# Expert weights through one ring of nine 2 MB slots in place of head and tail buffers of 1 MB, in a transformer layer with a top-4-of-32 mixture of experts

## What is computed

```python
def expert_block(args):
    xb, e = args
    g = xb @ w_gate[e] + b_gate[e]
    u = xb @ w_up[e] + b_up[e]
    g = jnp.minimum(g, SWIGLU_LIMIT)
    u = jnp.clip(u, -SWIGLU_LIMIT, SWIGLU_LIMIT)
    a = g * jax.nn.sigmoid(SWIGLU_ALPHA * g) * (u + 1.0)
    return a @ w_down[e] + b_down[e]
```

## Time and profile before

| | |
|---|---|
| median of 3 runs | 1187.4 us (1185.58 to 1191.16) |
| the profiled execution, own time | 1189.11 us |
| its span in the profile | 1187.2 us |
| TensorE busy | 1116.5 us, 94% |
| DVE busy | 306.2 us, 26% |
| ACT busy | 199.2 us, 17% |
| DMA, all queues | 438.73 MB, 370 GB/s over the span |

### The profile page before, as it was taken

The page is one execution under the profiler, slowest core; times in us unless marked ns, Lnnn a source line. Parts: engine busy times, 40 slices in busy tenths (PEclk is TensorE's granted clock), DMA queues, the critical chain, the costliest instruction groups (busy, mean ns, idle before and its releaser), DMA issues.

```text
span 1187.2 us, 13964 instructions
## 1 busy us (share of the span) xinstructions
PE 1116.5 (94%) x5368; PEld 523.6 (44%) x5368; DVE 306.2 (26%) x719; ACT 199.2 (17%) x339; POOL 5.5 (0%) x12
## 2 busy tenths in 40 slices
PE   7999999999999999999999999999999999999996
PEld 5888888533433333333333333333333333333332
DVE  7666665431111111111111111111121111111112
ACT  5345443011111111110111111101111111111111
POOL 1000000000000000000000000000000000000000
PEclk9999999999999999999999999999999999999998
DMA  9644327889999999799999999999999999999995
GB/s 351 230 168 152 121 94 289 363 332 378 421 421 421 421 422 421 282 423 421 423 422 422 421 422 421 423 421 422 421 423 421 423 421 423 421 423 421 423 421 213
DMA packets 71923, 438.73 MB, mean 370 GB/s; under 512 B 7356, under 2 KB 8408, under 8 KB 22744
## 3 DMA queue, kind: packets, MB, share of 16 engines
q1 hardware_dynamic: 71880, 438.36, 90.2%
q10 hardware_dynamic: 16, 0.00, 0.0%
HBM read 437.29 MB, written 1.05 MB: 369 GB/s over the span
## 4 chain that ended last, share of the span: by engine, by line
PE 82%; DMA 12%; ACT 3%; issue 1%; DVE 1%; SPq 0%; POOL 0%; DVEq 0%; POOLq 0%; ACTq 0%
PE ps L874 48%; DMA wu<-in_w_up_dram 11%; PE ps L901 5%; PE ps L838 4%; PE ps L862 4%; PE ps L598 4%; PE ps L784 2%; PE ps L636 2%; PE ps L661 2%; PE ps L628 2%; ACT gates L541 1%; PE ps L708 1%; PE ps L709 1%; PE ps L710 1%; DMA xs<-in_x_dram 1%
## 5 line engine op out<-in xcount | busy, mean ns | idle before, releaser
L874 PE MATMUL ps<-wd,o_t 128*64 128x512 f32 x1024 | 228.5, 598 | 22.8 <-issue 12.5
L874 PE MATMUL ps<-wu,gates 128*64 128x512 f32 x640 | 146.1, 594 | 6.2 <-DMA wu<-in_w_up_dram 6.2
L1264 DVE TENSOR_SCALAR gates<-ps 128x512 f32<-128x512 f32 x32 | 22.1, 692 | 486.9 <-PE ps L874 486.9
L874 PEld LDWEIGHTS ps<-wd,o_t 128*64 128x64 f32 x1024 | 78.6, 137 | 150.5 <-issue 137.4
L874 PE MATMUL ps<-wg,gates 128*64 128x512 f32 x512 | 113.0, 592 | 0.0
L874 PEld LDWEIGHTS ps<-wu,gates 128*64 128x64 f32 x640 | 50.1, 137 | 96.3 <-issue 75.6
L874 PE MATMUL ps<-attn,gates 128*64 128x512 f32 x384 | 89.3, 600 | 0.0
L553 ACT ACTIVATE gates<-ps 64x512 f32<-64x512 f32 x64 | 37.9, 592 | 233.1 <-PE ps L874 232.3
L874 PEld LDWEIGHTS ps<-wg,gates 128*64 128x64 f32 x512 | 43.3, 137 | 66.5 <-issue 64.0
L901 PE MATMUL ps<-gates,o_t 128*128 128x512 f32 x128 | 59.2, 605 | 10.2 <-ACT o_t L537 8.9
L862 PE MATMUL ps<-bias_tab,work 128*64 128x512 f32 x256 | 67.1, 595 | 0.7 <-DVE gates L1258 0.7
(11 more groups left out here) (163 smaller groups left out, 1083.8 us busy)
## 6 DMA issues: line engine op xcount, KB each, us to landing
wd<-in_w_down_dram SPq DMA_DIRECT2D x128, 1024.0 KB, 15.0
wu<-in_w_up_dram SPq DMA_DIRECT2D x80, 1024.0 KB, 22.3
wg<-in_w_gate_dram SPq DMA_DIRECT2D x64, 1024.0 KB, 17.5
attn<-in_w_gate_dram SPq DMA_DIRECT2D x32, 1024.0 KB, 18.9
v_tok<-in_w_gate_dram SPq DMA_DIRECT2D x16, 1024.0 KB, 21.8
work<-in_w_gate_dram SPq DMA_DIRECT2D x16, 1024.0 KB, 23.6
xn<-in_w_up_dram SPq DMA_DIRECT2D x16, 1024.0 KB, 25.5
attn<-in_w_up_dram SPq DMA_DIRECT2D x16, 1024.0 KB, 25.8
```

The lines of the kernel that those rows point to most:

```text
L874: mm = pe.matmul(ps[SLOTS * h:SLOTS * h + SLOTS, bank, :], lhs[:, k, :], w[:, k - 2 * j, 512 * h:512 * h + 512], start=(k == 0 and not bia ...
```

## The change

The 19 places of 1 MB become a ring of nine slots of 2 MB (18 MB): `attn[:, 2048:6144]`; the end of `work` and the start of `v_tok`, which now lie side by side; the halves of `wg`, `wu` and `wd`; and `xn` with `h_t`. A piece is 2 MB, 6 for an expert, two for each matrix. Piece number n of all 192 goes to slot n % 9, is issued in the order of use, and waits only until piece n - 9 is used. Partition p holds four successive rows of a matrix, 16 KB in one run (`RUN = 4`); the DMAs number half as many.

With four rows in a partition the transposes take every fourth column, a step of 4 floats (`every_fourth`), in `turn_rows`, `turn_residual` and for `rows_f`; their number is the same. The waits of DVE and ACT on `pieces_used` are rewritten in the new pieces: that for `pick_biases` is met when half of the up product is done (2 MB), where it was a quarter (1 MB). The loops over the pairs are unrolled on TensorE, DVE and ACT, and SP's loops too; the waits there are on constants. `g_fin` is loaded to `attn[:, 0:1024]` before the router's logits are done, and the result is written to `wg`.

```diff
-PIECES = 12
-HEAD = 7
-AHEAD_PAIRS = 4
+PIECES = 6
+RING = 9
+RUN = 4
...
+        work_at = nc.sbuf_base + (-nc.sbuf_base) % 32
         work = sb("work", [P, 4608])
+        v_tok = sb("v_tok", [P, NB, 1280])
+        slot_wv = nc.alloc_sbuf_tensor_at("slot_wv", [P, RUN, D], F32, offset=work_at + 2560 * 4)
+        slot_xh = nc.alloc_sbuf_tensor_at("slot_xh", [P, RUN, D], F32, offset=xn_at)
...
-        g_fin = msk[:, 0:D]
+        g_fin = attn[:, 0:D]
+        y_out = wg[:, 0:NB, :]
...
+        ring = [attn[:, 8 * SEQ:24 * SEQ].rearrange("p (k c) -> p k c", c=D), slot_wv]
+        ring += [t[:, 4 * j:4 * j + 4, :] for t in (wg, wu, wd) for j in range(2)] + [slot_xh]
+
+        def every_fourth(ap, r):
+
+            return ap[:, :].rearrange("p (c r) -> p r c", r=RUN)[:, r, :]
...
-        expert_v = [t[0].rearrange("e (j p r) f -> e j p r f", p=P, r=2) for t in (w_gate, w_up, w_down)]
+        expert_v = [t[0].rearrange("e (j p r) f -> e j p r f", p=P, r=RUN) for t in (w_gate, w_up, w_down)]
...
+            def piece(n, e):
+
+                m, j = n % PIECES // 2, n % 2
+                sp.dma_start(ring[n % RING][:], expert_v[m][e, j]).then_inc(ld_ring[n % RING], 16)
...
             sp.wait_ge(row_max, n_soft[N_UNITS])
-            piece(1, 1, 1)
+            piece(0, 0)
             sp.wait_ge(pv_done, N_UNITS // 2)
-            piece(2, 1, 1)
-            piece(3, 1, 1)
+            piece(1, 0)
...
             sp.wait_ge(oproj_done, KT)
...
+            for n in range(2, 6):
+                piece(n, 0)
+            for n in range(6, 8):
+                sp.wait_ge(wo_used, 2 * (n - 5))
+                piece(n, 1)
+            sp.dma_start(g_fin, ln_final_g.rearrange("(a d) -> a d", a=1).broadcast_to([P, D])).then_inc(ld_gfin, 16)
             sp.wait_ge(logit_done, NB)
...
+            piece(8, 1)
+            for n in range(RING, E * PIECES):
+                sp.wait_ge(pieces_used, n - RING + 1)
+                piece(n, n // PIECES)
...
-                    at = 512 * h + 2 * P * (k // 2)
-                    mm = turn(ps[:, 6 + h, P * k:P * k + P], every_second(xs[:, b, at:at + 2 * P], k % 2))
+                    mm = turn(ps[:, 6 + h, P * k:P * k + P], every_fourth(xs[:, b, 512 * h:512 * h + 512], k))
...
             def turn_rows(bank, rows_ap):
                 for j in range(4):
-                    mm = turn(ps[:, bank, P * j:P * j + P], every_second(rows_ap[:, 2 * P * (j // 2):2 * P * (j // 2) + 2 * P], j % 2))
+                    mm = turn(ps[:, bank, P * j:P * j + P], every_fourth(rows_ap, j))
                 return mm
...
+                for j in range(2):
+                    n = (E if again is not None else e) * PIECES + 2 * m + j
+                    pe.wait_ge(ld_ring[n % RING], (n // RING + 1 if again is None else again + (n // RING + 1)) * 16)
+                    for r in range(RUN):
+                        k = RUN * j + r
                         for h in range(2):
                             mm = pe.matmul(ps[SLOTS * h:SLOTS * h + SLOTS, bank, :], lhs[:, k, :],
-                                           w[:, k - 2 * j, 512 * h:512 * h + 512],
+                                           ring[n % RING][:, r, 512 * h:512 * h + 512],
                                            start=(k == 0 and not bias), stop=(k == KT - 1), skip_group_check=True)
                     mm.then_inc(pieces_used, 1)
...
-            with pe.Fori(1, E // 2 - 1) as i:
+            for i in range(1, E // 2 - 1):
                 pair(i)
...
-                    dve.wait_ge(pieces_used, n * PIECES + 5)
+                    dve.wait_ge(pieces_used, n * PIECES + 3)
```

More of the change, by code:

```diff
@@ L219, in layer @@
         ld_wo, ld_wout, ld_gfin, ld_bdn = sem("ld_wo"), sem("ld_wout"), sem("ld_gfin"), sem("ld_bdn")
-        ld_main = [sem(f"ld_main{q}") for q in range(PIECES)]
-        ld_second = [sem(f"ld_second{q}") for q in range(HEAD)]
+        ld_ring = [sem(f"ld_ring{s}") for s in range(RING)]
         wo_used = sem("wo_used")
@@ L368, in _ @@
             sp.wait_ge(oproj_done, KT)
-            piece(4, 1, 1)
-            for q in range(7):
-                piece(q, 0, 0)
-            for q in range(8, PIECES):
-                sp.wait_ge(wo_used, q - 7)
-                piece(q, 0, 0)
-            piece(5, 1, 1)
-            sp.wait_ge(logit_done, NB)
-            piece(6, 1, 1)
-            def head(i, item):
-                for q in range(HEAD):
-                    sp.wait_ge(pieces_used, i * (2 * PIECES) + ((item - 2) * PIECES + q + 1))
-                    piece(q, i, item % 2, first=item, step=2)
-            def tail(i, item):
-                for q in range(HEAD, PIECES):
-                    sp.wait_ge(pieces_used, i * (2 * PIECES) + ((item - 1) * PIECES + q + 1))
-                    piece(q, i, item % 2, first=item, step=2)
-            with sp.Fori(0, AHEAD_PAIRS) as i:
-                head(i, 2)
-                tail(i, 1)
-                head(i, 3)
-                tail(i, 2)
-            tail(AHEAD_PAIRS, 1)
-            with sp.Fori(AHEAD_PAIRS + 1, E // 2) as i:
-                for item in range(2):
-                    head(i, item)
-                    tail(i, item)
-            sp.wait_ge(pieces_used, (E - 1) * PIECES + HEAD)
-            sp.dma_start(g_fin, ln_final_g.rearrange("(a d) -> a d", a=1).broadcast_to([P, D])).then_inc(ld_gfin, 16)
+            for n in range(2, 6):
[4 more added lines that the diff above has]
+            sp.dma_start(g_fin, ln_final_g.rearrange("(a d) -> a d", a=1).broadcast_to([P, D])).then_inc(ld_gfin, 16)
+            sp.wait_ge(logit_done, NB)
+            piece(8, 1)
+            for n in range(RING, E * PIECES):
+                sp.wait_ge(pieces_used, n - RING + 1)
+                piece(n, n // PIECES)
             sp.wait_ge(over_ready, 1)
@@ L645, in _ @@
                     turn(ps[:, 7, 0:24], rows[:])
-                    for r in range(2):
-                        mm = turn(ps[:, 7, 24 + 4 * r:28 + 4 * r], every_second(rows_f, r))
+                    for r in range(RUN):
+                        mm = turn(ps[:, 7, 24 + 2 * r:26 + 2 * r], every_fourth(rows_f, r))
                     mm.then_inc(rows_turned, 1)
@@ L854, in turn_activation, with product @@
                 turn_rows(G, a_rows).then_inc(a_turned, 1)
-            def product(m, heads, tails, side, bank, lhs, bias=True):
+            def product(m, e, bank, lhs, bias=True, again=None):
                 if bias:
@@ L938, in pair @@
                     pe.wait_ge(a_t_ready, n + 1)
-                    down(n, i + 1, side)
+                    down(n)
                     if side == 0 and first:
@@ L959, in _ @@
                     turn_gathered(n)
-                    gate_and_up(n, k + (E // 2 + 1), 0)
+                    gate_and_up(n, again=k)
                     turn_activation(n)
                     pe.wait_ge(a_t_ready, n + 1)
-                    down(n, k + (E // 2 + 1), 0)
+                    down(n, again=k)
                     turn_selection(k + (E // 2 + 1), n * 2 + 2)
@@ L1321, in _ @@
             pair(0, first=True)
-            with dve.Fori(1, E // 2 - 1) as i:
+            for i in range(1, E // 2 - 1):
                 pair(i)
```

63 lines of the change are left out of this document (18 added, 45 removed).

## The result

| | before | changed |
|---|---|---|
| median | 1187.88 us (1185.58 to 1191.16, 4 runs) | 1177.95 us (1177.17 to 1178.41, 4 runs) |
| span of the profiled execution | 1187.2 us | 1176.5 us |
| ratio | | 0.9922, 95% interval 0.9909 to 0.9935 |

The changed kernel is 0.8% faster. The forecast was 1210.9 us, slower; what came is rival A (1178.3 us), to 0.4 us. That it came so near is partly luck: single executions of before lie 5.6 us apart (1185.58 to 1191.16), and the fastest of each kernel differ by 8.4 us, the medians by 9.9.

The account below looks back on a forecast made before the run. TensorE was taken to set the pace up to about 860 us, then the DMA engines. Weight waits -9.15 and transposes +32.6 gave +23.5 us on 1187.4, so 1210.9 us; range 1178 to 1217, likeliest case 1202 to 1219.

Parts of the forecast that it names:

- rival A: Transposes at a step of 4 cost what a step of 2 costs, leaving the weights' gain: 1178.3 us; chance 0.25.
- The step of the transposes: TensorE's 272 transposes, read at a step of 4 in place of 2, take 0.12 us more each: +32.6 us.
- rule of 16-byte stretches: Transposes' weight load goes by stretches touched: 32 in about 60 ns, 64 in 120, 128 in 240 at steps 1, 2, 4.
- second link: At a step of 2 the transposes' load bounds them, so whatever a step of 4 adds reaches the path in full.
- -9.15 us for waits on weights: Ring and larger runs together remove TensorE's waits for weights in the five late pairs: -9.15 us.
- The rate with runs of 16 KB: Weight DMAs in 16 KB packets move 428 GB/s in place of 421; the last piece lands near 1147 us.
- the ring: Nine weight slots, refilled in order of use, bring 5.5 of the 9.15 us even at the old DMA rate.
- Unrolling at nothing: Straight code in place of the loops costs no time that shows; some tenths of a us a pair if that failed.
- The small items: DVE's later wait, SP's issues, `g_fin` moved ahead, result in `wg`, last down product: no cost counted.
- Rivals B and C: B: added load partly hidden or 20 to 60 ns, 1189 us, 0.06; C: 16 KB runs cut up or slower, 1195, 0.04.

Follow-up runs that it names:

- e1_steps: Changed kernel with a probe behind its work, reading operands at steps of 1 to 64 floats; transposes came 109 ns apart at 1, 120 at 2 and 4.
- e2_step1: Changed kernel with adjacent columns (step of 1) in the experts' 256 transposes, output not the layer's; 1176.45 us, ratio 0.9914 to the kernel before.
- e3_runs8k: Changed kernel with runs of 8 KB and transposes at a step of 2, ring and straight code kept; 1186.63 us, ratio 0.9995 to the kernel before.
- e8_loop8k: Changed kernel with runs of 8 KB and the loops put back, ring kept; 1184.43 us, ratio 0.9975 to the kernel before.
- e5_unrolled: Kernel before with only the pair loops of TensorE, ACT and DVE unrolled; 1191.21 us, ratio 1.0039 to the kernel before.

## Why the prediction was wrong

1. *The step of the transposes, +32.6 us: wrong, and it alone decided the sign.* I drew a line through two points (140 ns at a step of 1, 209 at 2) by a rule of 16-byte stretches and read +120 ns off it at a step of 4. The changed kernel has 211 ns there and e1_steps 209, and the eight transposes take the same 0.96 us: the term is 0. The 60 ns that the line had at a step of 1 stood in no row either; e1_steps has the transposes 109 ns apart there. Two points fit a line and a stair alike, and the rival that said so had 0.25. The row of DVE that I took against that rival compared two different operations, on another engine and at a step of 32. DVE does pay for a step of 4 (273 ns against 226), but on TensorE's weight load that said nothing.

A second link of the same term was wrong too: that at a step of 2 the load is the bound, so that whatever is added to it is added to the path in full. The transposes are on the path, but of 69 ns less load e2_step1 shows 0.22 us / 16 = 14 ns for each, and from a step of 16 to 64 the load grows by 66 ns and the spacing by 34. By that ratio 120 ns more of load would have cost some 60 ns a transpose and not 120, half of the 32.6 us (an estimate from these two rows).

The rule of the Trainium skill that stood behind my line ("SBUF — State Buffer", section "Door 1: The DMA port swizzle": two hits in a 16-byte line) is what the moving operand does (0.45 us at a step of 2, 0.91 at 4), not the stationary one (206 and 209 ns in e1_steps). The Trainium skill's other page ("Vector Engine (DVE) Microarchitecture Reference", 5.2: pairs, and any hop between them is free) gives the stationary operand's stair, but for DVE itself the trace has 235 ns at a step of 2 against 226 at 1 and 261 at 3, so most of the stair stands one step later than its pairs would put it.

2. *-9.15 us for waits on weights: right.* 296.45 us became 287.36, five times 57.47, in the one trace of each kernel.

3. *The rate with runs of 16 KB: right.* 428 GB/s was forecast from two packet sizes, 427 to 429 came. It was needed more than I thought: I gave the ring 5.5 of the 9.15 us at the old rate; it had none as unrolled (e3_runs8k) and 2 to 4 with loops (e8_loop8k: 1184.43 against 1188.01 by medians, 2.2 us in the table). I had counted bytes and a mean rate, and let every transfer land with all its parts at once: the last piece was to land near 1147 us, and its last parts come near 1155.

4. *Unrolling at nothing: right for TensorE, wrong for the DMA engines.* The row that I took for it lies in the mixer stage, where the DMA share is 0.40. It could show that TensorE is not held up, and it was not. It could not show what straight code costs where the DMA engines are full: 4 to 5 us (e5_unrolled). In the changed kernel this is covered, with little to spare: the last parts of the last transfer arrive near 1155 us, and TensorE reaches them at 1154.87 + 3.4 = 1158.3.

5. *The small items: right, one unexplained.* DVE waits longer at the later signal and shorter behind it; waits by line, the bias pick and the up half of the activation:

```profile
DVE work L1182 <- PE ps L835: 68.6, 31, 2.2
DVE gates L1231 <- PE ps L835: 67.4, 32, 2.6
```

The second was 124.0 us before: part of the slack is used, and 2.1 us for an expert are left. SP issues the first refill at 247.96 us (forecast 247.9). The last down product is the same 8.80 us, of which the prediction did not see that 1.7 are the lower clock, and `g_fin` and the result's new place leave no mark in the chain.

6. *Rivals B and C* did not occur: no load time was added that could have been half hidden, and 16 KB runs were neither cut up nor slower.

## What to carry to other kernels

A price seen at two settings does not give the third: with two mechanisms that agree on both points, look up which operand and engine each was seen on, and give them like chances. Where an engine draws on a stock that another resource fills, read the margin of both, since what is free to the one (straight code and its fetches) is charged to the other. And ask of each transfer when its last part lands, not what the mean rate is.

## What the runs showed of the hardware

- TensorE's stationary operand in f32: 140 ns for 128 columns in order, 193 to 211 ns (medians) at any step from 2 to 32, 262 at 64. Its moving operand: 0.43 us for 512 columns at a step of 1, 0.45 at 2, 0.91 at 4, 0.86 at 16. Why the one pays at 2 and the other at 4 stays open.
- ACT's copy of 512 columns out of PSUM: 597 ns written in order, 1037 with neighbours written 128 floats apart.
- Packets of 16 KB move 428 GB/s, of 8 KB 421.5, as 10 ns a packet and 0.0368 ns a byte would have it.
- Instructions are fetched by the DMA engines that carry the data, in packets of 16 KB (0.70 MB in 43). When those engines are full, straight code with 26 more of them costs 4 to 5 us, and straight code on an idle engine 17 us by medians and 20 in the traces. The Trainium skill's page "Runtime: NRT & Kernel Launch" (section "Instruction fetch mechanics") has the blocks of 16 KiB and the queue, holds the fetch for hidden by the pace of the instructions, and takes unrolling for the cheaper form. By the traces that is so only as long as the engine that computes sets the pace.
